# mLSTM core: two gate blocks between a pair's scores and its numerators, three buffers of scaled numerators, other PSUM banks for the last numerators

## The reference

```python
def mlstm_mixer(u, w_in, conv_w, conv_b, gate_b, w_out):
    z = u @ w_in
    qk = jax.nn.silu(causal_conv(z[..., :2 * A_QK], conv_w, conv_b))
    v = z[..., 2 * A_QK:2 * A_QK + A_V]
    og = z[..., 2 * A_QK + A_V:2 * A_QK + 2 * A_V]
    gates = z[..., 2 * A_QK + 2 * A_V:] + gate_b
    ...
    hs = mlstm_scan(...)
    y = from_blocks(hs) * jax.nn.sigmoid(og)
    return y @ w_out

# one step of the scan: s are the weighted scores, hb the head's output
    s = jnp.einsum('bhld,bhsd->bhls', qb, kb) * w_intra
    num = jnp.einsum('bhls,bhsv->bhlv', s, vb) + ...
    den = jnp.sum(s, axis=-1) + ...
    hb = num / jnp.maximum(jnp.abs(den), jnp.exp(-m))[..., None]
```

## Time and profile before

| | us |
|---|---|
| median of 3 runs | 822.7 |
| lowest, highest | 822.55, 823.04 |
| the profiled execution | 822.93 |
| its span in the profile | 821.0 |
| TensorE busy, matmuls | 804.1 (98%) |
| TensorE busy, weight loads | 780.0 (95%) |
| VectorE busy | 585.8 (71%) |
| ScalarE busy | 417.7 (51%) |
| GpSimd busy | 130.2 (16%) |

### The profile page before, as it was taken

How to read it: one execution, slowest core, us unless ns; L and a number is a source line. 1 busy time by engine, 2 the same in 40 slices (tenths; PEclk the granted TensorE clock), 3 DMA queues, 4 the chain that set the end, 5 groups by cost and what they waited for, 6 DMA issues and landing times.

```text
span 821.0 us, 15756 instructions
## 1 busy us (share of the span) xinstructions
PE 804.1 (98%) x6452; PEld 780.0 (95%) x6452; DVE 585.8 (71%) x945; ACT 417.7 (51%) x717; POOL 130.2 (16%) x138
## 2 busy tenths in 40 slices
PE   9999999999999999999999999999999999999996
PEld 9999999999899898989999999999899998899995
DVE  6877776797687875798777768776667567567643
ACT  7444444544257664655444445536555454464541
POOL 3000000122210000020000003130245202036413
PEclk9999999999899999999999999999999999999999
DMA  8876776676245633449878875536444551835521
GB/s 330 314 256 227 243 249 230 233 259 205 89 134 188 209 104 103 154 154 334 304 277 270 289 246 180 192 92 210 160 144 142 168 179 48 261 129 156 154 77 52
DMA packets 45770, 158.91 MB, mean 194 GB/s; under 512 B 5075, under 2 KB 7635, under 8 KB 45699
## 3 DMA queue, kind: packets, MB, share of 16 engines
q1 hardware_dynamic: 45698, 157.92, 57.5%
HBM read 156.83 MB, written 1.06 MB: 192 GB/s over the span
## 4 chain that ended last, share of the span: by engine, by line
PE 80%; DVE 12%; ACT 5%; issue 2%; POOL 1%; DVEq 0%; ACTq 0%; POOLq 0%
PE ps L112 73%; PE ps L114 7%; DVE w L114 3%; DVE u L114 2%; ACT w L114 2%; DVE tmp L114 2%; DVE yg L114 1%; DVE cv L114 1%; ACT SW L114 1%; POOL rst L114 1%; ACT L114 1%; ACT ytm L114 1%; DVE Vs L114 0%; DVE hT L114 0%; DVE g L114 0%
## 5 line engine op out<-in xcount | busy, mean ns | idle before, releaser
L112 PE MATMUL ps<-u,w 128*128 128x256 f32 (+1 forms) x3887 | 502.0, 286 | 2.5 <-DVE w L114 1.2
L112 PEld LDWEIGHTS ps<-u,w 128*128 128x128 f32 x3887 | 483.7, 189 | 11.2 <-DVE w L114 3.2
L114 DVE TENSOR_TENSOR w<-raw,w 128x1024 fp32r<-128x1024 f32 x245 | 298.1, 1227 | 161.1 <-ACT w L114 160.1
L114 ACT CAST w<-raw 128x1024 fp32r<-128x1024 f32 x245 | 253.9, 1049 | 124.9 <-PE ps L114 116.5
L112 PE MATMUL ps<-h,w 128*128 128x272 f32 (+1 forms) x1000 | 130.4, 285 | 0.0
L112 PEld LDWEIGHTS ps<-h,w 128*128 128x128 f32 x1000 | 126.1, 188 | 0.1
L114 POOL TENSOR_TENSOR sqa<-sqa,sq 128x256 f32<-128x256 f32 (+1 forms) x22 | 22.7, 1031 | 357.5 <-ACT sq L114 357.0
L114 POOL TENSOR_SCALAR Sb<-Sb,st 128x256 f32<-128x256 f32 x32 | 45.0, 1422 | 89.1 <-DVE st L114 89.1
L114 DVE SCALAR_TENSOR_TENSOR acc<-adr,cact,acc 128x1024 f32<-128x1024 f32 x42 | 56.6, 1358 | 0.2 <-DMA adr<-wada 0.2
L114 PE MATMUL ps<-u,w 128*128 128x256 f32 (+1 forms) x169 | 48.1, 285 | 0.0
L112 PE MATMUL ps<-m,w 128*128 128x256 f32 x368 | 46.7, 281 | 0.0
(11 more groups left out here) (175 smaller groups left out, 698.1 us busy)
## 6 DMA issues: line engine op xcount, KB each, us to landing
raw<-wst SPq DMA_DIRECT2D x245, 512.0 KB, 4.6
adr<-wada SPq DMA_DIRECT2D x48, 512.0 KB, 4.2
Bt<-bias_rows SPq DMA_DIRECT2D x8, 192.0 KB
hT<-xT SPq DMA_DIRECT2D x4, 272.0 KB, 5.1
outT<-hT SPq DMA_DIRECT2D x2, 384.0 KB, 2.6
outT<-hT SPq DMA_DIRECT2D x1, 256.0 KB, 2.6
cs<-cst SPq DMA_DIRECT2D x1, 140.0 KB, 5.0
cs<-cst SPq DMA_DIRECT2D x1, 128.0 KB, 6.9
```

The lines of the kernel that those rows point to most:

```text
L112: fn()
L114: fn().then_inc(m[0], m[1])
```

## The change

- One more gate block stands ahead: G(1) is recorded before the loop, and the loop records G(h+2). So two gate blocks, G(h+1) and G(h+2), lie between a pair's scores and S(h).
- The last heads: O(5) is recorded behind S(7), no longer between G(7) and S(6). In `head`, O(6) and O(7) stand behind the second and fourth inner tile (before: first and third).
- `ytm` and `den` have three buffers, not two.
- S(6) writes bank 5 and S(7) bank 7, in place of banks of the rotation. V(6) uses a bank of the rotation, in place of bank 4. The transposes of the gate rows (`acol`, `emc`) use bank 6 in place of bank 5.

```diff
--- before.py
+++ after.py
@@ -896,7 +896,7 @@
         vT = sb("vT", [P, 2, T], F32, ax)
         Vs = sb("Vs", [P, 3, NH, 130], F32, ax)
         SW = sb("SW", [P, 4, 640], F32, ax)
-        ytm = sb("ytm", [P, 2, 2, P], F32, ax)
+        ytm = sb("ytm", [P, 3, 2, P], F32, ax)
         og = sb("og", [P, NH, S], F32, ax)
         y1 = sb("y1", [P, NH, S], F32R, ax)
         y2 = sb("y2", [P, NH, S], F32R, ax)
@@ -907,7 +907,7 @@
         e3 = sb("e3", [72, 8], F32R, ax)
         acol = sb("acol", [P, 3, 8], F32, ax)
         emc = sb("emc", [P, 2, 8], F32, ax)
-        den = sb("den", [P, 2, 4], F32, ax)
+        den = sb("den", [P, 3, 4], F32, ax)
         ax.close()
         m_ffn = (pe.sem, pe.n)
         pe_done = m_ffn
@@ -939,7 +939,7 @@
 
         def v_transpose(h, mv):
             i = h % 2
-            bt = take() if h == NH - 1 else 4 + i
+            bt = take() if h >= NH - 2 else 4 + i
             pe.wait(mv, free[bt])
             for j, (a, e) in enumerate(tok_tiles(T)):
                 f = (partial(nc.tensor.transpose, ps[0:e - a, bt, 128 * j:128 * j + 128],
@@ -1008,23 +1008,23 @@
             b, m = block(x1[:, :, 16:T], x2[:, :, 16:T], S)
             ogm[h] = free[b] = act(partial(nc.scalar.activation, og[:, h, :], ps[:, b, 0:S], ACT.Tanh, scale=0.5), m)
 
-        pe.wait(m_a, free[5], gm["m"])
+        pe.wait(m_a, free[6], gm["m"])
         for j, (a, e) in enumerate(tok_tiles(T)):
-            mt = pe(partial(nc.tensor.transpose, ps[0:e - a, 5, 8 * j:8 * j + 8], t1[:, a:e],
+            mt = pe(partial(nc.tensor.transpose, ps[0:e - a, 6, 8 * j:8 * j + 8], t1[:, a:e],
                             cs[0:8, C_ID:C_ID + 8]))
         for t in range(2):
-            mt = pe(partial(nc.tensor.transpose, ps[:, 5, 32 + 8 * t:40 + 8 * t], rows[:, 1, 128 * t:128 * t + 128],
+            mt = pe(partial(nc.tensor.transpose, ps[:, 6, 32 + 8 * t:40 + 8 * t], rows[:, 1, 128 * t:128 * t + 128],
                             cs[0:8, C_ID:C_ID + 8]))
-        dve(partial(nc.vector.tensor_copy, acol[:, 0:2, :], ps[:, 5, 0:16].rearrange("p (j h) -> p j h", h=8)), mt)
-        m_ac = dve(partial(nc.vector.tensor_copy, acol[0:16, 2, :], ps[0:16, 5, 16:24]))
-        m_em = free[5] = act(partial(nc.scalar.activation, emc[:, :, :],
-                                     ps[:, 5, 32:48].rearrange("p (t h) -> p t h", h=8), ACT.Exp, scale=-1.0), m_ac)
+        dve(partial(nc.vector.tensor_copy, acol[:, 0:2, :], ps[:, 6, 0:16].rearrange("p (j h) -> p j h", h=8)), mt)
+        m_ac = dve(partial(nc.vector.tensor_copy, acol[0:16, 2, :], ps[0:16, 6, 16:24]))
+        m_em = free[6] = act(partial(nc.scalar.activation, emc[:, :, :],
+                                     ps[:, 6, 32:48].rearrange("p (t h) -> p t h", h=8), ACT.Exp, scale=-1.0), m_ac)
         m_em = dve(partial(nc.vector.tensor_scalar, emc[:, :, :], emc[:, :, :], 2.0, None, ALU.mult), m_em)
 
         mk = cs[:, C_MASK:C_MASK + 272]
 
         COL = [(0, 0, 0, 256, 128), (368, 368, 112, 256, 128), (256, 624, 240, 256, 16)]
-        swr, swm, yw, num, ytr = [None] * 4, {}, {}, {}, [None, None]
+        swr, swm, yw, num, ytr = [None] * 4, {}, {}, {}, [None] * 3
         dve.wait(m_msk)
 
         def weights(k):
@@ -1063,7 +1063,8 @@
         def sums_over_keys(h):
 
 
-            i, i2, b = h % 4, h % 2, take()
+
+            i, i2, b = h % 4, h % 3, (take() if h < NH - 2 else 5 + 2 * (h % 2))
             pe.wait(swm[h], Vm[h], free[b])
             for t, parts in enumerate(((0, 256), (128, 384, 512))):
                 for j, c in enumerate(parts):
@@ -1083,7 +1084,7 @@
 
         def output(h):
 
-            i2 = h % 2
+            i2 = h % 3
             pe.wait(num[h], free[6])
             for t in range(2):
                 m = pe(partial(nc.tensor.transpose, ps[:, 6, 128 * t:128 * t + 128], ytm[:, i2, t, :], ident))
@@ -1102,25 +1103,27 @@
                                 ALU.subtract), a)
 
         pend_y, yw1 = [], {}
+
         gate_block(0)
         weights(0)
+        gate_block(1)
+        v_transpose(*pend_v.pop())
         for h in range(NH):
-            if h < NH - 1:
-                gate_block(h + 1)
-            if h == 0:
-                v_transpose(*pend_v.pop())
-            elif h < NH - 1:
+            if h < NH - 2:
+                gate_block(h + 2)
+            if 0 < h < NH - 2:
                 output(h - 1)
             sums_over_keys(h)
             if h % 2 == 0 and h < NH - 2:
                 weights(h // 2 + 1)
+        output(NH - 3)
         ustate["use"] = swr[3]
         ygm = {}
 
         def last_outputs(i):
-            if i in (1, 3):
-                output((6, 7)[i // 2])
-            elif i == 4:
+            if i in (2, 4):
+                output(5 + i // 2)
+            elif i == 5:
                 low_y()
 
         def evac_mix(gain, ygm, paired=True):
```

## The result

| | before | changed |
|---|---|---|
| median us (6 runs each) | 822.75 | 819.89 |
| lowest, highest | 822.55, 823.09 | 819.13, 820.42 |
| profiled execution | 822.93 | 819.84 |
| its span | 821.0 | 817.9 |

The ratio is 0.9963, with a 95% interval from 0.9953 to 0.9973: 2.9 us faster. 819.9 was predicted.

What follows compares the result with a forecast made beforehand. Two limits in the core: TensorE's work and the ScalarE-VectorE loop. One round out (4.12 us), one split in (1.14), O(5) waiting 1.05: the product starts 2.76 us earlier, 822.7 to 819.9 us; range 818.8 to 821.3.

Steps and rivals of the forecast that it cites:

- TensorE's own work: Core up to the product: 36.19 us of matmul work without waits, so at most 3.81 us to win.
- Step 1: G(2) ahead of S(0): one more split on VectorE makes head 0's denominators and the loop behind 1.14 us late.
- Steps 2 and 3: Loop: den 0 to `ytm` of head 5 stays 26.25 us; the last round, 4.12 us, goes; 2.98 net.
- Step 4: S(6) in bank 5, S(7) in bank 7: none of the banks holds the product up; wait taken as 0.
- Step 5: O(5) waits 1.05 us for `ytm` of head 5, replacing 1.54 at the product, which starts at 316.97.
- Step 6: Bank 4 at W(0): the 0.97 us wait for V(6) goes, and S(0)'s too, adding nothing to the sum.
- Step 7: Third buffers of `den` and `ytm`: cost and hold up nothing; with two, head 7 would wait for O(5).
- Step 8: Behind O(5): `og` of head 5 near 317.2, in time for the product's sixth inner tile, 6.0 us behind 316.97.
- first rival: The loop doesn't hold O(5) up and TensorE is the limit throughout: 818.9 us; chance 0.09.
- Nothing is given back behind the core: Second rival claimed the opposite: gain lost to waits behind the core, half 821.3, all 822.7 us; chance 0.08.
- The third one: Rival: ScalarE must wait for TensorE ahead of the tanh of G(3) to G(7), giving 826.2 us; chance 0.04.
- its 5.14: By the skill's weight-load rule the core has 5.14 us to give, time down to 817.6; chance 1 in 100.

Runs made afterwards that it cites:

- o6_bank_4: o5_in_product with O(6)'s transposes in bank 4 in place of bank 6; 818.99 us, ratio 0.9953 to the kernel before.
- more_vector_work: The changed kernel with three idle VectorE products of 128x272 between G(2)'s split and the denominators of head 0; 821.50 us, ratio 0.9985.
- rotation_for_last: The changed kernel with S(6) and S(7) back in the rotating banks; 820.95 us.
- old_banks_4_5: The changed kernel with V(6) back in bank 4 and the gate rows back in bank 5; 820.12 us, ratio 0.9967.
- banks_only: The kernel before with only S(6) moved to bank 5 and S(7) to bank 7; 822.37 us, ratio 0.9993.
- o5_in_product: The changed kernel with O(5), O(6) and O(7) behind the product's second, third and fourth inner tiles; 820.38 us.

## Why the prediction was right

- *TensorE's own work*, 36.19 us, bounds the core: right as a sum. With the last waits removed (o6_bank_4) the core takes 35.99 without O(5), and the gain is 3.83 by the medians and 3.71 by the trace; 3.81 was given as the most. The terms are another matter, see the last point.
- *Step 1, the split ahead of head 0:* 1.14 late; 1.16 measured. G(2)'s tanh, at 287.62, waited for nothing. That the kernel pays for VectorE's work here is shown by more_vector_work.
- *Steps 2 and 3, the rounds:* den 0 to `ytm` of head 5 took 26.26 us (289.34 to 315.60); 26.25 was taken. That the last round fell out is in the order and in the six `ytm` in a row. rotation_for_last puts 2.39 of 2.83 us on the order. The gate block moved ahead and O(5) moved behind S(7) were not tried apart, so how the 2.39 divide between them is worked out, not shown.
- *Step 4, the banks:* no wait at S(6) or S(7), as said. What these banks bring on top of the order is 0.44 us; the prediction didn't separate it.
- *Step 5, O(5):* reached at 315.44 by the working (315.70 - 0.26), 315.51 measured; a wait of 1.05 us by the working, 0.91 measured. From `ytm`'s start to O(5) 0.82 us, not 0.92. Why it was 0.92 at the product's start before is open: in rotation_for_last the product again waits for three banks, of which S(6)'s comes last, and starts only 0.81 us behind the `ytm` that frees it (316.55 to 317.36). The product was due at 316.71 (316.97 - 0.26) and started at 316.62.
- *Step 6, bank 4:* worth nothing in the sum, and old_banks_4_5 shows just that, with the wait at O(5) gone.
- *Step 7, the third buffers:* no wait at S(7) for them. They weren't tried alone. That head 7 would have waited for O(5) with two buffers is wrong by the code: S(7) is recorded ahead of O(5), so its scaling would have had only O(3) to wait for, and would have overwritten numerators that O(5) still reads.
- *Step 8, behind O(5):* `og` of head 5 near 316.9 (317.2 - 0.26), 316.90 measured; no wait in the product. The trap that lies there, bank 6 behind the weight split, the working of this step would have shown: I followed head 5's data to the sixth inner tile and not the bank to the next output. In this change it costs nothing: O(5)'s `og` stands ahead of the split, and O(7) comes two inner tiles behind O(6). In two experiments it took the gain, 0.7 of some 1.1 us in banks_only and all of it in o5_in_product.
- *Terms that were off and cancel:* V takes 0.25 us in the changed kernel (283.77 to 284.02), not 0.49; the difference was S(0)'s wait, 0.41 by starts, which I had taken at the modelled 0.17. W(0) takes 1.35, not 1.44. Three S in a row take 3.27, not 3.12. And O(3), which follows G(6), came 3.07 us behind its start (303.31 to 306.38), where 2.90 would do: a part of the old gap of 0.25 remained, and the prediction had TensorE wait at O(5) alone. Too much by 0.33, too little by 0.32; with small differences in the gate blocks TensorE came to O(5) 0.07 us later than worked out. So that this term fits so well is in part luck. The time hangs on it little, since `ytm` is what O(5) waits for.

The rivals. The loop does hold O(5) up: without that wait the time is 819.0, near the 818.9 of the first rival. Nothing is given back behind the core (490.08 and 490.07 us). The third one's mechanism exists: in old_banks_4_5, where TensorE is 1 us later, ScalarE waits 0.46 us for G(2) ahead of its tanh, but still has 1.35 us of idle time behind it, until den 0 is there:

```profile
286.03 1.04 ACT L114 CAST w<-raw 128x1024 fp32r<-128x1024 f32 x1
287.53 0.38 ACT L114 ACTIVATE og<-ps 128x256 f32<-128x256 f32 x1 [0.46 <-PE ps L114]
289.26 0.77 ACT L114 ACTIVATE ytm<-ps,den 128x128 f32<-128x128 f32 x2 [1.35 <-DVE den L114]
```

The Trainium skill (Perfetto Trace Analysis, Identifying the Most-Contended Engine) judges TensorE's headroom by the busy share of its weight loads, beside its rate of arithmetic. In o6_bank_4 that leaves 35.99 - 34.42 = 1.57 us idle in a stretch in which the profile shows no wait of TensorE. Over this mix of transposes and narrow matmuls the rule says too much, by about the difference between its 5.14 and the 3.83 that could be had.

## What to carry to other kernels

- Where two engines hand work to and fro in a fixed order, look for the loop and count its rounds; both may be idle a quarter of the time or more (here 24% and 33% of the core) and still be the limit. What counts is how many rounds lie ahead of the instruction that TensorE waits for.
- An early wait of TensorE is worth nothing when it later waits for such a loop anyway. Two short probes, idle work on the one engine and then on the other, tell which is the limit, as long as the idle work is shorter than the wait.
- When an output is moved, follow its bank to the next user and not only its data. A bank's release that stands behind a long unrelated instruction (here a split of 1.14 us) can cost as much as late data.

## What was not expected of the hardware

The three VectorE products of 128x272, each dependent on the one before by a semaphore, took 1.32 us, 0.44 each; I had counted with 0.34, the step from `og` to `y` (316.90 to 317.24), which don't depend on each other in this way. They are of 128x256, so the wider tile has some part in it, and how much the dependence has was not measured. And the idle time that a profile puts before a matmul can be 0.24 us less than what by the starts is lost (0.67 against 0.91 at O(5), 0.17 against 0.41 at S(0) before), since the matmul before it is drawn longer than it holds the engine: at O(3) (306.38) 0.15 us are lost and none is shown.
